# The prompt stage's value pages are asked for by GpSimd's queue instead of SyncE's

## The reference

```python
z = jnp.einsum('bqhd,bshd->bhqs', qi, kf) * Dh ** -0.5 + bias
mask = kpos[None, :] < pi[:, None]
l1mb = jnp.where(mask, jax.nn.log_sigmoid(-z), 0.0)
after = lax.cumsum(l1mb, axis=3, reverse=True) - l1mb
A = jnp.where(mask, jnp.exp(jax.nn.log_sigmoid(z) + after), 0.0)
return jnp.einsum('bhqs,bshd->bqhd', A, vf)
...
k_past = cache_sb_k[l][page_table].reshape(DB, past, SB_HEADS, SB_DIM)
v_past = cache_sb_v[l][page_table].reshape(DB, past, SB_HEADS, SB_DIM)
```

## Time and profile before

| | |
|---|---|
| median of 3 timed runs | 1549.67 us (1547.23 to 1550.81) |
| profiled execution, its own time | 1545.77 us |
| its span in the trace | 1544.1 us |
| mean granted TensorE clock | 0.913 of full speed |
| busy: PE, DVE, ACT, POOL | 1281.7, 855.3, 481.0, 357.4 us |
| DMA, share of 16 engines: SyncE's queue, GpSimd's | 46.8%, 2.1% |

### The profile page before, as it was taken

The page is one execution under the profiler, slowest core; times in us unless marked ns, Lnnn a source line. Parts: engine busy times, 40 slices in busy tenths (PEclk is TensorE's granted clock), DMA queues, the critical chain, the costliest instruction groups (busy, mean ns, idle before and its releaser), DMA issues. The chain is left out here.

```text
span 1544.1 us, 23048 instructions
## 1 busy us (share of the span) xinstructions
PE 1281.7 (83%) x7717; PEld 1073.5 (70%) x7717; DVE 855.3 (55%) x1192; ACT 481.0 (31%) x901; POOL 357.4 (23%) x235
## 2 busy tenths in 40 slices
PE   4577679889798854998988889599999997697997
PEld 4567557767676543888888788477777876366885
DVE  3245689888887532759779596243444443324221
ACT  4231245435445531232232413231313131322110
POOL 0029434424330000735434353000000000000000
PEclk8698789999899986999999999799999898898999
DMA  4446657557473423655354642475646452543320
GB/s 150 143 151 191 186 160 242 180 175 245 142 231 111 150 77 95 216 160 182 107 179 128 213 151 70 142 238 153 205 141 207 152 158 71 196 136 110 109 82 28
DMA packets 200276, 237.89 MB, mean 154 GB/s; under 512 B 13395, under 2 KB 122290, under 8 KB 200154
## 3 DMA queue, kind: packets, MB, share of 16 engines
q1 hardware_dynamic: 196194, 224.60, 46.8%
q0 software_dynamic: 3968, 11.87, 2.1%
HBM read 215.87 MB, written 20.64 MB: 153 GB/s over the span
## 5 line engine op out<-in xcount | busy, mean ns | idle before, releaser
L1979 POOL TENSOR_TENSOR bp_keys<-bp_keys,bp_q 128x1024 f32<-128x1024 f32 x64 | 156.4, 2465 | 171.7 <-DMA bp_keys<-cache_sb_k 163.9
L1979 POOL TENSOR_TENSOR cp_keys<-cp_keys,cp_q 128x1024 f32<-128x1024 f32 x64 | 161.5, 2542 | 142.9 <-DMA cp_keys<-cache_sb_k 139.7
L150 PE MATMUL bank<-xh,b_w_hi 128*128 128x344 f32 x480 | 163.0, 340 | 31.0 <-DVE b_w_lo L133 27.1
L150 PE MATMUL bank<-xl,b_w_hi 128*128 128x344 f32 x480 | 158.8, 331 | 0.0
L150 PE MATMUL bank<-xh,b_w_lo 128*128 128x344 f32 x480 | 158.4, 330 | 0.0
L150 PE MATMUL bank<-xh,d_w_hi 128*128 128x344 f32 x384 | 130.8, 341 | 26.0 <-ACT d_w_hi L128 18.3
L244 PE MATMUL bank<-xh,c_w_hi 128*128 128x344 f32 x384 | 130.6, 340 | 9.2 <-ACT c_qT L250 4.6
L244 PE MATMUL bank<-xh,c_w_lo 128*128 128x344 f32 x384 | 126.7, 330 | 0.0
L244 PE MATMUL bank<-xl,c_w_hi 128*128 128x344 f32 x384 | 126.7, 330 | 0.0
L150 PE MATMUL bank<-xl,d_w_hi 128*128 128x344 f32 x384 | 125.9, 328 | 0.0
L150 PE MATMUL bank<-xh,d_w_lo 128*128 128x344 f32 x384 | 125.8, 328 | 0.0
(11 more groups left out here) (376 smaller groups left out, 2603.1 us busy)
## 6 DMA issues: line engine op xcount, KB each, us to landing
cp_keys<-cache_sb_k SPq DMA_DIRECT2D x128, 256.0 KB, 2.8
cp_values<-cache_sb_v SPq DMA_DIRECT2D x128, 256.0 KB, 2.8
bp_keys<-cache_sb_k SPq DMA_DIRECT2D x128, 256.0 KB, 3.1
dp_values<-cache_sb_v SPq DMA_DIRECT2D x128, 256.0 KB, 3.0
b_w_raw<-w_in SPq DMA_DIRECT2D x20, 512.0 KB, 4.9
c_w_raw<-w_in SPq DMA_DIRECT2D x16, 512.0 KB, 5.1
d_w_raw<-w_in SPq DMA_DIRECT2D x16, 512.0 KB, 5.3
o_mix<-mix SPq DMA_DIRECT2D x8, 1024.0 KB, 5.9
```

The costliest lines, as they stand in the source:

```text
L150: last = self.nc.tensor.matmul(self.bank(j, c)[:, 0:self.width], w[:, s, k, :], x[:, k, c * self.width:(c + 1) * self.width], start=(k == ...
L1979: self.nc.gpsimd.tensor_tensor(self.keys[:, s], self.keys[:, s], q, ALU.mult).then_inc(self.scaled.sem, 1)
```

## The change

`load_values` moves from SyncE's program into GpSimd's. The pages, the ring, the semaphores and the waits are the same. Pairs 0 to 3 of sequence 0 are asked for ahead of the first product; those of a later sequence behind the product of `r == 1` of its own round; pairs 4 and 5 behind the product of `r == 8`, 6 and 7 behind 9, 8 and 9 behind 11, 10 and 11 behind 12, 12 and 13 behind 14, 14 and 15 behind 15. SyncE keeps keys, queries, tiles and stores in their order.

```diff
--- before.py
+++ after.py
@@ -602,12 +602,7 @@
                 if i < GT:
                     keys.load_query(sp, i)
 
-            def load_values(i, first, end):
-                for r in range(first, end if i < GT else first):
-                    values.load_values(sp, i, r, keys.page_ids)
-
             values.setup_sync(sp)
-            load_values(0, 0, 4)
             for i in range(GT):
                 load_keys(i + 1, 4, 6)
                 load_tile(4 * i + 5)
@@ -617,29 +612,22 @@
                 sp.dma_start(k.sb_v_prompt[:, :, i * P:(i + 1) * P], v_tok[:]).then_inc(v_out, 16)
                 load_keys(i + 1, 9, 10)
                 load_tile(4 * i + 6)
-                load_values(i, 4, 6)
                 sp.wait_ge(tok_taken, 5 * i + 3)
                 sp.sem_inc(sending, 1)
                 sp.dma_start(k.sb_k_sample[:, i * P:(i + 1) * P], new_tok[:, 0]).then_inc(new_out, 16)
                 sp.dma_start(k.sb_v_sample[:, i * P:(i + 1) * P], new_tok[:, 1]).then_inc(new_out, 16)
                 load_keys(i + 1, 10, 12)
-                load_values(i, 6, 8)
                 sp.wait_ge(tok_taken, 5 * i + 5)
                 sp.sem_inc(sending, 1)
                 sp.dma_start(k.sb_k_prompt[:, :, i * P:(i + 1) * P], k_tok[:]).then_inc(k_out, 16)
                 load_keys(i + 1, 12, 13)
-                load_values(i, 8, 10)
                 load_keys(i + 1, 13, 15)
                 load_tile(4 * i + 7)
-                load_values(i, 10, 12)
                 load_keys(i + 1, 15, NP)
-                load_values(i, 12, 14)
                 load_query(i + 2)
                 load_keys(i + 2, 0, 2)
-                load_values(i, 14, NP)
                 load_tile(4 * i + 8)
                 load_keys(i + 2, 2, 4)
-                load_values(i + 1, 0, 4)
             sp.wait_ge(v_out, 16 * GT)
             sp.wait_ge(k_out, 16 * GT)
             sp.wait_ge(new_out, 32 * GT)
@@ -827,6 +815,12 @@
                 columns = slice(half * W, (half + 1) * W)
                 pool.dma_start(k.mix_dram[i + 2 * GT, :, columns], mix[:, columns]).then_inc(mix_out[half], 16)
 
+            def load_values(i, first, end):
+                for r in range(first, end if i < GT else first):
+                    values.load_values(pool, i, r, keys.page_ids)
+
+            behind = {8: (4, 6), 9: (6, 8), 11: (8, 10), 12: (10, 12), 14: (12, 14), 15: (14, NP)}
+            load_values(0, 0, 4)
             for i in range(GT):
                 for r in range(NP):
                     if r == 5 and i:
@@ -835,6 +829,10 @@
                         store(i, 0)
                     if i + 1 < GT:
                         keys.multiply_keys(pool, i + 1, r)
+                    if r == 1 and i:
+                        load_values(i, 0, 4)
+                    if r in behind:
+                        load_values(i, *behind[r])
             store(GT - 1, 1)
             pool.wait_ge(mix_out[0], 16 * GT)
             pool.wait_ge(mix_out[1], 16 * GT)
```

## The result

The changed kernel is slower: 1560.3 us in the median of 7 runs (1556.35 to 1566.23), beside 1547.2 (1544.35 to 1551.20, 7 runs) for the kernel before on the same chip. The ratio is 1.0085, 95% interval 1.006 to 1.0109, or 13 us (9 to 17). Forecast was 1547.2 with a range of 1540 to 1559, so it lies just above the range. The profiled execution has a span of 1563.9 us (before 1544.1). Of these 19.8 us, 12.3 lie in the stage and at its end, 2.5 ahead of it and 5.0 behind it; one pair of executions differs by more than the medians do.

What follows compares the result with a forecast made beforehand. The prediction took TensorE to set the pace. Value waits -4.0, round 3 0 and the start +1.5 gave -2.5 us: 1543.3 from the profiled 1545.8, or 1547.2 in timed runs' terms; range 1540 to 1559.

Steps and rivals of the forecast that it cites:

- The value waits of rounds 0 and 1 go, -4.0 us: Rounds 0 and 1: TensorE's three waits for value pages, 3.96 us together, would vanish; -4.0 us.
- A pair costs GpSimd 2.54 us, and all fits between the products: GpSimd, rounds 0 to 2: 1.38 us of reads plus two 0.58 us issues per pair, with 3.8 us left at the tightest.
- The rival of GpSimd as the bound: Third to sixth block of rounds 0 to 2: above 3.0 us a pair GpSimd limits, 1559 to 1563.5 us; chance 0.20.
- Hidden reads: GpSimd's page-number reads cost nothing, a pair 1.16 us, waits in all rounds go: -10.8 us, 1538.9; chance 0.17.
- Round 3, 0: Round 3, no products: GpSimd's chain ends at 548.3, SyncE's at 548.58; 0 us (-5.3 if reads are free, +11 if double).
- The start of round 0, +1.5, between -1.5 and +4: Four pairs ahead of GpSimd's first product delay it to about 177.6 and VectorE's reductions by 2.8 us; +1.5 us taken.
- Products moved against scans elsewhere, counted as nothing: Rounds 0 to 2: products stay near their old places and stall VectorE as before; new-token waits stay near 6 us; 0 us.

Runs made afterwards that it cites:

- e9: The changed kernel, with pairs 4 to 15 of round 3 asked for by SyncE as before; 1562.2 us, ratio 1.008.
- e7: The changed kernel, with the four pairs of round 0's start asked for behind product 3 instead of ahead of product 0; 1554.5 us, ratio 1.004.
- e6: The kernel before, with the odd pairs from 7 on of round 3 alone asked for by GpSimd; 1549.1 us, ratio 0.9983.
- e1: The changed kernel, with the four pairs at the start of round 0 asked for by SyncE again; 1552.8 us, ratio 1.0026.
- e2: The kernel before, with only the four pairs at the start of round 0 asked for by GpSimd, ahead of product 0; 1558.8 us, ratio 1.0059.
- e3: The kernel before, no page moved, GpSimd's first product held back by 18 memsets of an unused tile; 1553.5 us, ratio 1.0022.
- e4: The kernel before, with pairs 4 to 15 of every round on GpSimd at the changed kernel's places; 1560.0 us, ratio 1.0061.
- e11: The changed kernel, round 0's four pairs behind product 3, store ahead of product 7, round 3's pairs from 4 on split between SyncE and GpSimd; 1541.0 us, ratio 0.9946.

## Why the prediction was wrong, step by step

*The value waits of rounds 0 and 1 go, -4.0 us:* the waits went, and none is left in rounds 0 to 2, but the time did not. From unit 4 of round 0 to unit 4 of round 3 the kernel after takes 2.2 us more than before, and e9, with the same program there, 0.4 us more. What took the place of the waits is under the last step below.

*A pair costs GpSimd 2.54 us, and all fits between the products:* right in size, 2.40 us ahead of the first product, and in the later blocks often less, because the sequencer reads numbers while a product runs (in e7 the loads of the page numbers stand beside products). The rival of GpSimd as the bound did not come: its condition was 3.0 us a pair. Hidden reads came in part, but not in round 3, where nothing hides them.

*Round 3, 0:* right, +0.6 us. One queue's chain of reads and requests sets the pace there, whichever queue it is (e9); two queues take 4 us off (e6).

*The start of round 0, +1.5, between -1.5 and +4:* this is the step that failed first. It measured +6.3, beyond the upper bound, and e1, e2, e3 and e7 all put it on that one place. The text had the late products (177.6 forecast; 178.3 measured, on the clock of the trace before) and the late reductions (end at 183.6 forecast, 184.3 measured), and it said that the burst would then stand beside the scans of units 1 and 2; but it priced that at the reductions' delay, 2.8 us, and took 1.5 of it. The path was wrong too: it led the delay to TensorE's wait for the turned values (c_v_tok, 5.6 us), which in fact shrank to 1.7, while TensorE waited 9.0 us for c_AT behind the scans; only in e3, where the operations come out one by one, is the long wait the one for c_v_tok. One thing was at hand and not used: the scans behind the reductions were due at 180.8, well inside the burst. The rows that show what can follow were even cited, two scans at 11.66 us beside four products. Held to the end of a burst of four from 177.6, the scans end at 187.9 in place of 182.0, 5.9 us late; with the burst of six that came, at 192, 10 us late. These are estimates from the rows, and TensorE's other waits take part of them up: in the kernel after the scans end 11.4 us late, and the start is 6.3 us longer. A term of 6 us instead of 1.5 would have made the forecast about 1552. The granted clock, which no term held, goes with the wait, but e9 shows that the start is as long without most of it.

The Trainium skill's SBUF — State Buffer (Who interferes with whom) says that a VectorE instruction with two SBUF inputs contends with a GpSimd instruction that reads SBUF; its Summary: rules for kernel authors says that the second to issue blocks fully until the first is done. The direction agrees: scans and the c_A multiplies stall (9.19 us for two in the kernel after, 5.03 in e3), reductions of one input do not (1.22 us inside the burst). The length agrees where the burst does not stand directly behind a DMA request: one product each, 2.5 to 2.8 us in e3. Directly behind a request it is another: there a scan waits to the end of the burst, 8.6 us for one here and 10.5 of the 11.66 us in the earlier trace rows.

*Nothing at the stage's end:* it was not a term at all, and it is +3.2 us, the drain. Its records in thirteen kernels show this, with 8.6 and 9.2 us in e4 and e9. The gap behind the stage grew with it each time.

*Products moved against scans elsewhere, counted as nothing:* this is the other step that failed. The prediction named it as what would prove it wrong, and it did happen, in both directions. In rounds 1 and 2 the pages put ahead of product 2 brought products 2 and 3 beside the scans of unit 1:

```profile
282.65 5.07 DVE L725 TENSOR_TENSOR_SCAN c_left<-c_keep,ones 128x128 f32<-128x128 f32 x2 [1.25 <-ACT c_keep L667]
...
289.91 0.27 PE L2125 MATMUL bank<-ones,cp_y_rows 128*128 128x1 f32 x1 [1.24 <-DVE cp_y_rows L2119]
```

and products 10 and 11 hold a scan of 128x256 in each of rounds 0 to 2:

```profile
236.96 3.71 DVE L725 TENSOR_TENSOR_SCAN c_left<-c_keep,ones 128x256 f32<-128x256 f32 x1 [1.89 <-ACT c_keep L667]
```

so the gate's c_mix is 1.3 us late three times. These bursts of two stand directly behind page requests, and the scans wait for both products. The 6.1 us of new waits eat up what the value waits (4.0) and c_new_tok (2.9 less in these rounds) gave. c_v_tok's 3.8 us less are not part of this; they lie at the start of round 0. That the new waits and the smaller c_new_tok waits come out so near each other is luck of where the products fall; e1 and e4 have c_new_tok waits of up to 7.7 us. Single parts of rounds 0 to 2 of e1 and e4 differ by up to 4 us from each other and from the changed kernel, which was not taken apart.

The sum, then: forecast -2.5, measured in the stage +12.3. Of the difference of 14.8, 4.8 are the start beyond its term, 3.2 the drain, 0.6 round 3, and 6.2 the way between: +2.2 in place of -4.0 from unit 4 of round 0 to unit 4 of round 3. By e9's trace in place of the changed kernel's that last term is 4.4; the other 1.8 us go with the lower clock of one execution.

The experiments point to a version better than both: the kernel before with the store ahead of product 7 (e5), 0.9932 (0.9905 to 0.9958). With pages on GpSimd as well, e11 comes to 0.9946 (0.9927 to 0.9964), which the measurement can't tell from it. So the move of the pages is worth nothing that can be measured, even where its start and round 3 are mended and the drain is shorter.

## What to carry to other kernels

Work put in front of a queue of products does not only delay them: if the engine that frees their buffers now works beside them, the buffers refill while they run, and they come as a longer burst. For each such burst, list the operations of the other engine that it holds up and that are due inside it. Price each at one product more; where the burst stands directly behind a DMA request of GpSimd, price the first at the end of the burst. Before a difference of a few microseconds between two traces is put down to a cause, look for another trace with the same program in that place. And when requests move to GpSimd's queue, look at the next barrier behind them as well as at the place where they are made.

## What the runs showed of the hardware

- GpSimd's drain at the end of a stage took 0.082 us for each DMA that it had asked for in that stage, 0.71 us after 8 and 9.2 us after 112; after 122 to 136 it was 2.8 to 3.9 us, and why is open.
- VectorE operations with two SBUF inputs waited for GpSimd's products. Where the products did not stand directly behind a DMA request of GpSimd, one VectorE operation was let in behind each product, at 89 of 89 places in thirteen traces (2.5 to 2.8 us for one in e3). Directly behind a request it was let in at 1 of 117, and a scan stood still to the end of the burst (8.6 us through four products, 10.5 us beside four). VectorE's reductions were not held (1.22 us).
- Two page numbers read by GpSimd cost 1.26 us where nothing ran beside them, and down to nothing behind products (eight issues in 4.32 us); the issue itself 0.54 us.
- The 9 us wait of TensorE was followed by a granted clock of 0.50 in the slice from 194 to 200 us and of 0.58 once more from 212 to 218; the matmuls of the start were busy for 0.8 to 3.1 us more in the four kernels that have this wait, at starts of 53.3 to 54.4 us.
